# Hybrid S5 and attention step on one core: attention's query blocks in descending order and on other steps, the halved order of the last two tiles in one round only

## What is computed

```python
proj = rmsnorm(x, norm_g) @ w_in                 # 2048 -> 10240
u_a, z_a, q, k, v, z_b, g_a, g_b = split(proj)   # 1024 wide; g_a, g_b 2048 wide
y_a, h_last = s5_scan(u_a, ...)                  # 64 groups, complex state of 64
y_a = gelu(y_a); y_a = y_a * sigmoid(y_a @ glu_w + glu_b) * silu(z_a)
# attention, 8 heads of 128; for each block of 128 queries:
z = q_blk @ k.T * scale + bias                   # masked where key >= query
log_keep = -softplus(z)
later = reverse_cumsum(log_keep) - log_keep      # along the keys
w = exp(log_sigmoid(z) + later);  o = w @ v
out = x + (sigmoid(g_a) * (y_a @ w_a) + sigmoid(g_b) * ((o * silu(z_b)) @ w_b)) @ w_out
y = rmsnorm(out, norm_f)
```

## Time and profile before

| | |
|---|---|
| median of 3 runs | 3296.19 us (3294.12 to 3297.76) |
| the profiled execution | 3297.37 us |
| its span, first to last instruction | 3295.6 us |
| mean granted clock of TensorE | 0.981 |
| phase A, eight rounds | about 66 to 2391 us; a round takes 290 us, the last 294 |
| busy in the fourth round (936.5 to 1227.3, 290.8 us) | PE 281.42, DVE 74.90, ACT 97.37, POOL 84.67 us |

### The profile page before, as it was taken

The page is one execution under the profiler, slowest core; times in us unless marked ns, Lnnn a source line. Parts: engine busy times, 40 slices in busy tenths (PEclk is TensorE's granted clock), DMA queues, the critical chain, the costliest instruction groups (busy, mean ns, idle before and its releaser), DMA issues.

```text
span 3295.6 us, 51396 instructions
## 1 busy us (share of the span) xinstructions
PE 3165.0 (96%) x20712; PEld 3075.0 (93%) x20712; DVE 1006.3 (31%) x1343; ACT 1005.4 (31%) x1304; POOL 758.7 (23%) x2311
## 2 busy tenths in 40 slices
PE   5999999999999999999999999999899999999997
PEld 4999899899989989998998999899899999999997
DVE  5123113311321331132133113212555214332266
ACT  5215313421531342153135215313522101121142
POOL 5540450054045005404500550351012100000000
PEclk8999999999999999999999999999999989999999
DMA  4121122222212212221221122122247645342283
GB/s 131 57 88 59 56 64 84 64 59 80 66 55 65 84 60 64 69 78 54 66 85 59 51 69 90 48 64 87 96 148 249 200 156 177 110 128 70 70 233 113
DMA packets 375458, 305.29 MB, mean 93 GB/s; under 512 B 36466, under 2 KB 343234, under 8 KB 373186
## 3 DMA queue, kind: packets, MB, share of 16 engines
q1 hardware_dynamic: 375234, 302.10, 29.6%
HBM read 229.92 MB, written 67.93 MB: 90 GB/s over the span
## 4 chain that ended last, share of the span: by engine, by line
PE 63%; POOL 16%; DMA 5%; DVE 5%; issue 4%; SPq 3%; ACT 3%; POOLq 1%; DVEq 0%; ACTq 0%
PE acc L1618 51%; PE side L1585 4%; PE side L1771 3%; POOL work L1140 2%; POOL work L1138 2%; POOL work L1137 2%; POOL work L1139 2%; POOL work L1143 2%; DMA work<-t_qkv 1%; POOL work L1144 1%; DMA t_qkv<-stage 1%; PE side L1820 1%; DVE work L1384 1%; PE side L1766 1%; ACT w_high L779 1%
## 5 line engine op out<-in xcount | busy, mean ns | idle before, releaser
L1618 PE MATMUL acc<-x_high,w_high 128*128 128x344 f32 (+2 forms) x5440 | 1228.4, 329 | 11.7 <-issue 6.2
L1618 PE MATMUL acc<-x_low,w_high 128*128 128x344 f32 (+2 forms) x5440 | 1182.6, 321 | 0.0
L1618 PE MATMUL acc<-x_high,w_low 128*128 128x344 f32 (+2 forms) x5440 | 1178.8, 320 | 0.0
L1618 PEld LDWEIGHTS acc<-x_high,w_high 128*128 128x128 f32 x5440 | 912.0, 190 | 37.4 <-issue 24.5
L1618 PEld LDWEIGHTS acc<-x_low,w_high 128*128 128x128 f32 x5440 | 924.5, 189 | 0.0
L1618 PEld LDWEIGHTS acc<-x_high,w_low 128*128 128x128 f32 x5440 | 915.7, 189 | 0.0
L1310 DVE TENSOR_TENSOR w_low<-w_raw,w_high 128x1024 fp32r<-128x1024 f32 x233 | 295.7, 1269 | 991.8 <-ACT w_high L779 991.0
L779 ACT CAST w_high<-w_raw 128x1024 fp32r<-128x1024 f32 x232 | 243.2, 1048 | 1008.5 <-PE acc L1618 956.1
L1127 POOL COPY work<-s_tables 128x28 f32 x16 | 3.7, 228 | 1387.5 <-DMA work<-in_state_ssm_im 1387.5
L1585 PE MATMUL side<-work 128*128 128x128 f32 (+6 forms) x832 | 151.0, 306 | 3.5 <-DVE work L1377 3.5
L1585 PEld LDWEIGHTS side<-work 128*128 128x128 f32 (+3 forms) x832 | 100.9, 159 | 33.8 <-issue 25.6
(11 more groups left out here) (286 smaller groups left out, 2592.5 us busy)
## 6 DMA issues: line engine op xcount, KB each, us to landing
w_raw<-in_w_in SPq DMA_DIRECT2D x160, 512.0 KB, 4.0
w_raw<-in_w_out SPq DMA_DIRECT2D x48, 512.0 KB, 4.0
t_qkv<-stage SPq DMA_DIRECT2D x24, 516.0 KB, 5.0
work<-t_qkv SPq DMA_DIRECT2D x24, 516.0 KB, 4.2
work<-t_sig_ga SPq DMA_DIRECT2D x24, 516.0 KB, 4.6
out<-work SPq DMA_DIRECT2D x18, 512.0 KB
t_sig_gb<-stage SPq DMA_DIRECT2D x16, 516.0 KB, 4.3
t_sig_ga<-stage SPq DMA_DIRECT2D x16, 516.0 KB, 3.4
```

The lines of the kernel that those rows point to most:

```text
L1618: ins = mm(acc[s][:, a, 0:n], w[b][:, kk, :], x[:, kx, c0:c0 + n], start=start, stop=stop)
```

## The change

Attention's query blocks are taken from the widest (qb = 7) to the narrowest (qb = 0): `ROWS` pairs n = 0 to 7 with qb = 7 to 0, and step tables, semaphore counts and the double buffer go by n. All steps of SC, ST, WT and PV are new. K's transposes go from step 65 to 56 and wait for the first block's scores to be read; the second block's scores wait for K's copy. ZB's evacuation keeps step 57, by a name of its own. The order of `chunk_of` is halved in the last round only: in the others GA0 takes chunks 16 and 17 and is evacuated at step 72, and SP sends it behind chunk 19 of its own walk. For that, PE's phase A becomes a loop of 7 rounds and a last round written out (its variable `last` is renamed `last_op`).

```diff
-    def chunk_of(cn):
-        if cn < CHUNKS - 4:
+    def chunk_of(cn, last):
+        if cn < CHUNKS - 4 or not last:
             return cn // 2, cn % 2
         return ((GA0, 0), (GA1, 0), (GA0, 1), (GA1, 1))[cn - (CHUNKS - 4)]
...
-                if cn % 2 == 1 and cn > 1 and cn // 2 - 1 not in (U, ZB, GA0):
+                if cn % 2 == 1 and cn > 1 and cn // 2 - 1 not in (U, ZB, GA0)[0:3 if last else 2]:
                     send(cn // 2 - 1)
...
-            send(GA0)
+            if last:
+                send(GA0)
             oz_out()
             send(GA1)
...
-    VT, NTR, KTR = 52, 53, 65
-    SC = (54, 55, 58, 61, 64, 68, 72, 75)
-    ST = SC[1:] + (78,)
-    WT = (56, 59, 62, 66, 70, 74, 77, 79)
-    PV = tuple(p + 1 for p in WT[:7]) + (79,)
+    VT, NTR, KTR, ZB_AT = 52, 53, 56, 57
+    SC = (54, 57, 60, 63, 66, 69, 71, 73)
+    ST = SC[1:] + (75,)
+    WT = (58, 61, 64, 67, 70, 72, 74, 76)
+    PV = tuple(p + 1 for p in WT)
+    ROWS = tuple(enumerate(range(7, -1, -1)))
...
-                if p == 76:
-                    evacuate(i, GA0)
+                if p == (76 if last else 72):
+                    evacuate(i, GA0, last)
...
-                if p == PV[0]:
+                if p == ZB_AT:
                     evacuate(i, ZB)
...
-                for qb in range(8):
+                for n, qb in ROWS:
                     w = P * (qb + 1)
-                    if p == ST[qb]:
-                        act.wait_ge(arg_ready, 8 * i + qb + 1 + PRIMED)
-                        nc.scalar.activation(zb[qb % 2][:, 0:w], zb[qb % 2][:, 0:w], ACT.Exp).then_inc(w_ready, 1)
+                    if p == ST[n]:
+                        act.wait_ge(arg_ready, 8 * i + n + 1 + PRIMED)
+                        nc.scalar.activation(zb[n % 2][:, 0:w], zb[n % 2][:, 0:w], ACT.Exp).then_inc(w_ready, 1)
...
-        with pe.Fori(0, FT) as i:
+        def phase_a(i, last):
             for p in range(PTS):
                 cn = p // 4
-                t, half = chunk_of(cn)
+                t, half = chunk_of(cn, last)
...
                 if p == KTR:
-                    pe.wait_ge(z_ready, 8 * i + 5)
+                    pe.wait_ge(z_ready, 8 * i + 1)
...
-                for qb in range(8):
-                    if p == WT[qb]:
-                        pe.wait_ge(w_ready, 8 * i + qb + 1)
-                        if qb == 3:
-                            pe.wait_ge(ktok_ready, i + 1)
-                        elif qb < 7:
-                            pe.wait_ge(z_ready, 8 * i + qb + 2)
+                for n, qb in ROWS:
+                    if p == WT[n]:
+                        pe.wait_ge(w_ready, 8 * i + n + 1)
+                        if n < 7:
+                            pe.wait_ge(z_ready, 8 * i + n + 2)
                         else:
                             pe.wait_ge(oz_ready, 8 * i + 7 + PRIMED)
...
-                        if qb == 0:
+                        if n == 0:
                             pe.wait_ge(new_ready, i + 1)
-                        elif qb == 1:
-                            pe.wait_ge(z_ready, 8 * i + 1)
+                        elif n == 1:
+                            pe.wait_ge(ktok_ready, i + 1)
                         else:
-                            pe.wait_ge(oz_ready, 8 * i + qb - 1 + PRIMED)
+                            pe.wait_ge(oz_ready, 8 * i + n - 1 + PRIMED)
...
+        with pe.Fori(0, FT - 1) as i:
+            phase_a(i, False)
+        phase_a(FT - 1, True)
```

More of the change, by code:

```diff
@@ L378, in ahead @@
                 if cn + 2 < CHUNKS:
-                    t, half = chunk_of(cn + 2)
+                    t, half = chunk_of(cn + 2, last)
                     load_chunk(w_in[0], half * CK, bass.ds(weight_column(t, i), P), 0, b)
@@ L753, in _, with evacuate @@
         nc.scalar.copy(tab[:, :, :], side[:, 0, 0:7 * GROUPS].rearrange("p (a g) -> p a g", a=7)).then_inc(tab_ready, 1)
-        def evacuate(i, t):
-            act.wait_ge(chunk_used, i * CHUNKS + (CHUNKS - 1 if t == GA0 else 2 * (t + 1)) + PRIMED)
+        def evacuate(i, t, late=False):
+            act.wait_ge(chunk_used, i * CHUNKS + (CHUNKS - 1 if late else 2 * (t + 1)) + PRIMED)
             if t == U:
@@ L1646, in _ @@
                     k = half * CK + kk
-                    last = products(cn % 2, kk, k, t % 2, ALL, k == 0, k == KT - 1)
+                    last_op = products(cn % 2, kk, k, t % 2, ALL, k == 0, k == KT - 1)
                 if p % 4 == 3:
-                    last.then_inc(chunk_used, 1)
+                    last_op.then_inc(chunk_used, 1)
                 for hf in range(2):
@@ L1667, in _ @@
                             one(side[0:64, 0, b_:b_ + NEW], SR[:, g, 64:128], i8)
-                            last = one(side[64:128, 0, b_:b_ + NEW], SR[:, g, 0:64], negid[0:NEW, 0:NEW])
-                        last.then_inc(a_mm, 1)
+                            last_op = one(side[64:128, 0, b_:b_ + NEW], SR[:, g, 0:64], negid[0:NEW, 0:NEW])
+                        last_op.then_inc(a_mm, 1)
                     if p == BT[hf]:
@@ L1684, in _ @@
                         for g in range(HG):
-                            last = one(side[0:GC, 0, g * P:(g + 1) * P], M1[:, g, 0:GC], N1[:, g, 0:CH * GC])
-                        last.then_inc(k_mm, 1)
+                            last_op = one(side[0:GC, 0, g * P:(g + 1) * P], M1[:, g, 0:GC], N1[:, g, 0:CH * GC])
+                        last_op.then_inc(k_mm, 1)
                     if p == PQ[hf]:
@@ L1691, in _ @@
                             one(side[:, 0, g * P:(g + 1) * P], B1T[:, g, :], Ug[:, HG * hf + g, :])
[L1692 to L1693 removed]
+                            last_op = one(side[:, 1, g * P:(g + 1) * P], B2T[:, g, :], Ug[:, HG * hf + g, :])
+                        last_op.then_inc(pq_mm, 1)
                     if p == YM[hf]:
@@ L1705, in _ @@
                             a = 256 + g * NEW
-                            last = one(side[:, 1, a:a + NEW], B1T[0:GC, g, :], Us[:, HG * hf + g, :])
-                        last.then_inc(y_mm, 1)
+                            last_op = one(side[:, 1, a:a + NEW], B1T[0:GC, g, :], Us[:, HG * hf + g, :])
+                        last_op.then_inc(y_mm, 1)
                     if p == YS[hf]:
@@ L1712, in _ @@
                             one(side[0:NEW, 1, g * GC:(g + 1) * GC], hn[:, g, :], N1[:, g, 0:GC])
-                            last = one(side[0:NEW, 0, g * P:(g + 1) * P], hn[:, g, :], ident[:, :])
-                        last.then_inc(ys_mm, 1)
+                            last_op = one(side[0:NEW, 0, g * P:(g + 1) * P], hn[:, g, :], ident[:, :])
+                        last_op.then_inc(ys_mm, 1)
                 if p == XJ:
@@ L1729, in _ @@
                     for g in range(8):
-                        last = one(side[0:GC, 0, g * NEW:(g + 1) * NEW], ident[:, g * GC:(g + 1) * GC], uT[:, SEQ:TOK])
-                    last.then_inc(us_mm, 1)
+                        last_op = one(side[0:GC, 0, g * NEW:(g + 1) * NEW], ident[:, g * GC:(g + 1) * GC], uT[:, SEQ:TOK])
+                    last_op.then_inc(us_mm, 1)
                 if p == YT:
@@ L1753, in _ @@
                     for n, src in enumerate((qT, kT, vT)):
-                        last = one(side[0:NEW, 0, n * P:(n + 1) * P], src[:, SEQ:TOK], ident[:, :])
-                    last.then_inc(new_tr, 1)
-                for qb in range(8):
-                    if p == WT[qb]:
-                        pe.wait_ge(w_ready, 8 * i + qb + 1)
-                        if qb == 3:
-                            pe.wait_ge(ktok_ready, i + 1)
-                        elif qb < 7:
-                            pe.wait_ge(z_ready, 8 * i + qb + 2)
+                        last_op = one(side[0:NEW, 0, n * P:(n + 1) * P], src[:, SEQ:TOK], ident[:, :])
+                    last_op.then_inc(new_tr, 1)
+                for n, qb in ROWS:
+                    if p == WT[n]:
+                        pe.wait_ge(w_ready, 8 * i + n + 1)
+                        if n < 7:
+                            pe.wait_ge(z_ready, 8 * i + n + 2)
                         else:
```

86 lines of the change are left out of this document (43 added, 43 removed).

## The result

The changed kernel took 3324.19 us (median of four runs, 3318.01 to 3327.92), the kernel before 3295.68 us beside it. The ratio is 1.0084, 95% interval 1.0066 to 1.0102: slower by 28 us. The profiled execution took 3326.6 us, its span is 3324.8.

What follows compares the result with a forecast made beforehand. PE, busy 96% of the span, was taken as the bound. Seven rounds of -10.8 + 10.0 + 3.0 + 0.3 = +2.5 us made +17.5, so 3314 us; range 3288 to 3334.

Steps and rivals of the forecast that it cites:

- What the tail cost: From WT6 to the next round before the change: PE loses 10.8 us a round, all of which goes.
- New idle: Attention steps after the change: PE waits, mainly at PV0, PV2 and PV5, add 10.0 us a round.
- The clock: Half speed behind new idles costs 3.0 us a round: PV2 1.4, PV0 and PV5 1.1 each, less 0.6.
- The jump back: At PE's loop edge: two steps of products cover the jump, costing 0; bound 0 to 2.3 us a round.
- Round start: At step 3, POOL and the seeds may be later after ACT's final evacuation: 0.3 us a round taken.
- Last round: Written-out last round: PV5's wait goes, PV7 waits some 2.3 us behind ACT's y casts; no change in total.
- The sum: Seven rounds of phase A at +2.5 us each: +17.5 us, giving 3314 us.
- the first (half speed at PV2 alone): Rival: clock holds behind shorter idles, falling only at PV2: +0.9 us a round, 3302 us; chance 0.13.
- The second rival: ACT's evacuations at steps 64 and 72 fall into its own waiting: -5.2 us a round, 3260 us; chance 0.17.
- The third (the jump shows): Rival at PE's loop edge: the jump back costs 2.3 us more in seven rounds, 3330 us; chance 0.10.

Runs made afterwards that it cites:

- e3: Changed kernel with ACT's evacuation of GB1 moved from step 64 to 65, behind the copy for PV2: 3292.09 us, ratio 0.9993 to the kernel before.

## Why the prediction was right

The direction and the mechanism held: the tail's waits went, and waits for ACT's copy came at PV0, PV2 and PV5. The measured 28 us lie above the forecast's 17.5, inside its range. Step by step:

- **What the tail cost, 10.8 us a round.** All of its waits are gone from the trace after, and the term was about right. In the fastest version (no jump back, no half speed) the first seven rounds take 282.1 us on average against 290.4, and each still has five short waits of 1.6 us in all: 9.9 us, and some 0.8 more with what the profile's idle leaves out (next point).
- **New idle, 10.0 us a round.** Shown are 8.4 to 8.8: 0.25 (0.2 forecast) at WT0, 2.12 (2.5) at PV0, 0.26 to 0.63 (0.8), 3.02 (3.1), 1.98 (2.4), and twice 0.38 (0.5). The profile's idle leaves out the overlap that is lost: without a wait a group of matmuls starts some 0.16 us before the end of the one ahead (917.67 for an end of 917.83). At seven places that makes 9.5 to 9.9, so the term was right. The walk through the queues by durations of the trace before found every wait shown within some 0.5 us.
- **The clock, 3.0 us.** Right in its sum: 57.6 us of busy half speed are 28.8 us of loss, 3.6 a round (3.6 forecast, less 0.6 for later waits made shorter), and filling the idles gave back 25 us, 3.1 a round. In its parts it was wrong, so the sum is partly luck. I took the longest idle as the surest cause and gave PV5 1.1 us; but PV5's idle of 1.98 us was followed by half speed in all seven rounds, PV0's in four of eight and PV2's of 3.02 us in three of eight. Its source was also read too simply: of the seven falls before, six came behind an idle of 2.74 us and the last round's behind 5.6.
- **The jump back, 0.** This step failed. I argued from the output phase, whose loops show no gap, that two steps of products cover it; the trace shows 0.76 to 1.13 us ahead of six rounds, 5.9 us in all, and with cover the written-out version is 8.2 (traces) to 10.4 us (medians) faster. That is 6 to 10 us where phase A came out 5.2 us over the forecast's 17.5. The queue of 64 instructions that the Trainium skill gives PE (TensorE: Matmul & The Clock Gate, "Architectural detail") would by estimate have covered 5 us; the runs do not bear that sum out for this loop, whose body is 80 steps long. Why the output phase shows nothing was not tried.
- **Round start, 0.3.** Nothing: the wait for POOL is 0.80 us as before, and step 9 begins 27.8 us into a round in both kernels, where the clock is full at its start.
- **Last round, 0.** It came out 1.8 us shorter. The wait of 2.18 us at PV7 behind the y casts is there, as forecast (2.3).
- **The sum.** Measured in the seven rounds: +3.5 us each in place of +2.5, so +24.4, less 1.8 for the last: the 22.7 us of phase A. The terms as they turned out give -10.8 + 9.7 + 3.1 + 1.0 (jump) = +3.0 a round, which leaves 0.5 without a place. The rest of the 28 us is the clock in the decode stage of these executions, which no term had.

Of the rivals, the first (half speed at PV2 alone) is refuted by the trace: it came at all three places. What the Trainium skill's table of two states (TensorE: Matmul & The Clock Gate) says of the clock, that it falls after a whole idle window, does not foretell these falls. They came with idles of 1.98 to 3.02 us, and were gone when these were filled or taken away. The second rival (the evacuations fall into ACT's own waiting) is refuted by e3, where moving one of them took 2.3 us of wait away in each round. The third (the jump shows) was half right: it shows, at 6 to 10 us and not 16. The table load is followed at once by its user in the trace after as well (889.81 and 1.28 us, then 891.11). The drain that the Trainium skill (ScalarE: Activation LUTs, "What ACT_TABLE_LOAD costs") adds is not there; PV2's wait of 3.02 us fits the rows and not 5.9.

## What to carry to other kernels

When work is placed by hand between the steps of a busy engine, what decides is the cover between a producer's trigger and its consumer, counted in the producer's queue order: one evacuation placed in front of a copy cost 32 us here, and two changes, each harmless or good alone, lost 28 us together because one put an evacuation in front of a copy of the other that had no room for it (without it the descending version took 27 us less). A walk through the queues with the durations of one trace finds such places to half a microsecond, and the same walk finds steps that avoid them (57 us here). Count idles of TensorE like these, of 2 to 3 us, as dearer than they look, since the clock fell with 48 of 77 of them, and try writing out a long loop (10 us here).

## What the runs showed of the hardware that was not expected

- Half speed is not ordered by the length of the idle. Over the four traces that have such idles (the changed kernel, the order alone, GB1's evacuation moved, PE written out), a fall began in the idle or within some 2 us behind it in 17 of 32 cases at PV0 (2.10 to 2.16 us), in 14 of 24 at PV2 (3.02 us), and in 17 of 21 at PV5 (1.98 us). At PV5 it was 14 of 14 where PV2's idle of 3.02 us stood earlier in the round, and 3 of 7 where that had been cut to 0.69. PV5 also has a wait of 0.38 us two steps before it and another right behind. Which of these is the reason, if either, was not tried.
- The changed kernel had 15, and with PE's rounds written out and the same idles 20, half-speed stretches in phase A. The kernels with such idles spread over 9 to 18 us between runs, the three whose trace has no half speed in phase A over 2 to 5 us.
- More matmuls made the kernel faster: 6.6 us of useless work a round in place of idle gained 25 us.
- Writing out six more rounds in PE's program (some 1,870 matmuls a round, and as many weight loads) cost nothing that can be seen, and each jump back cost 1.4 to 1.7 us even with two steps of products behind the last product of attention.
